# Stick-breaking attention in pairs of heads, dilated units one tile ahead, other banks, constants behind the scratch

## The chip, the cores and the metric

The kernel runs on one core of a Trainium2 chip. Its time is the device time of one execution in microseconds (us); of the kernel before, three runs gave 2281.86, 2284.05 and 2284.53, median 2284.05. TensorE multiplies, VectorE (DVE) and ScalarE (ACT) do the elementwise work and read its results from PSUM, which has 8 banks of 512 fp32 words per partition; weights stream in by DMA.

## The reference

A first block (512 tokens, width 1024; projections, pooling, convolutions, a gated merge) is followed by a second one of two layers. Each layer projects, attends in two ways, merges by gates, and runs a feed-forward network. What the change touches:

```
z    = q @ k.T * scale                        # stick-breaking, 4 heads of 64
keep = where(key < query, log_sigmoid(-z), 0)
attn = where(key < query, exp(log_sigmoid(z) + suffix_sum(keep)), 0)
out  = attn @ v

# dilated: 4 head slots in 3 groups (window, stride) = (128,1), (512,4), (2048,16)
o_g, m_g, den_g = softmax attention of group g
out  = sum_g softmax_g(m_g + log(den_g)) * o_g
x    = x + (gates[:D] * (dil @ w_proj_a) + gates[D:] * (sb @ w_proj_b)) @ w_out
```

## The kernel before, in words

Each fp32 product is made of three fp32r passes: an operand is split into a high part (ScalarE, L453 for weights) and a low part (VectorE, L460), and lines 1597 to 1599 multiply high by high, high by low, low by high. A weight tile of 1024 x 128 is 24 such matmuls of 512 columns (`col_tile`); value projections go by `token_tile` with 48 of 256 columns. The order of the work is written out by hand, and each engine runs its own list in order; semaphores tie them. Weight pieces pass a ring of four slots (`whl`), so tile n + 3 is split while tile n is multiplied. Each layer has 18 tiles for the dilated q, k and v (`DIL_KEYS`, numbered n_ from 0), then 16 gate tiles, then the projections and the output rows. Attention is slipped in between tiles:

- Stick-breaking. Before, one head takes four tiles. Behind tile 0 `sb_scores` (L1807) writes z to banks 2 to 5; `sb_logs` on ScalarE takes abs, exp and log, `sb_softplus` on VectorE adds (L1445) and masks (L1447) them, ScalarE and VectorE split the result (L853, L1451); behind tile 2 `sb_exponents` (L1818) adds triangular sums to z; ScalarE exponentiates; behind tile 4 `sb_values` (L1830) makes the output in bank 6, and `sb_out` splits it into obT (L865, L1456) for `w_proj_b_2`. These fp32 matmuls run as two passes each, so the profile counts two for one.
- Rotation (`rope`, L1427 to L1437 on VectorE) of the 12 q and k tiles, which ScalarE copies out as qraw (L873).
- Dilated. A unit is two heads and 128 queries, eight units per layer, one for two gate tiles: `dil_scores` (L1856, L1860, banks 2 and 3), the maximum, `dil_exp` (L905), `dil_transposes` (L1871, banks 4 and 5), `dil_pT`, `dil_values` (L1889, banks 6 and 7). Groups 1 and 2 are held by class (every fourth token together), group 0 by token.
- `stat_rows` (L1905) turns maxima and denominators into rows, `shift_rows` and `share_rows` make the groups' shares, `share_wide` (L1917) spreads them over partitions, ScalarE copies them (L941), `dil_merge` (L1509 to L1511) applies them, and oaT (L1515) feeds `w_proj_a_2`. Its products are gated from PSUM (L1547), summed (L1549) and split; `row_tiles` then makes the output rows in banks 0 to 3 and 4 to 7.

`take` waits until a bank's last reader, which `give` has noted, is done.

Of the kernel before, what the change touches and what calls it, by code (L numbers as in the profile page):

```python
# [31 lines left out]
P = 128  # L32
D = 1024
SEQ = 512
# [67 lines left out]
def weight_plan():  # L102
# [34 lines left out]
    for l in range(LAYERS):  # L137
# [6 lines left out]
        for g in range(3):  # L144
            add("w_in_2", ("w_in_2v", l, 6 + g), [("dv", l, g, j) for j in range(2)], 1024)
# [12 lines left out]
def build(nc, t, out):  # L158
# [21 lines left out]
    PA_BANK = (2, 3, 4, 5, 0, 1, 6, 7)  # L180
# [3 lines left out]
    SBO = [0, 512, 896, 1152, 1280]  # L184
# [9 lines left out]
    def DIL_KEYS(l):  # L194
        return [(name, l, g, j) for name in ("dq", "dk", "dv") for g in range(3) for j in range(2)]

    count = 0
    for key in W:
# [5 lines left out]
        elif key[0] in ("dq", "dk", "gate"):  # L204
            W_BANK[key] = key[-1] % 2
        elif key[0] == "sv":
            W_BANK[key] = 4
        elif key[0] == "dv":
            W_BANK[key] = 4 if key[2] == 2 else 0
        elif key[0] in ("up_a", "up_b"):  # L210
            W_BANK[key] = (2 * key[2] + (key[0] == "up_b") * 2 - key[2] % 2) % 8


    base = (nc.sbuf_base + 63) // 64 * 64
# [13 lines left out]
    whl = keep("whl", [P, 4, 2, 1024], R)  # L228
    cst_at = at[0]
# [12 lines left out]
    arena = (at[0] + 127) // 128 * 128  # L242

    negtri_r = nc.alloc_sbuf_tensor_at("negtri_r", [P, P], R, offset=tri_at)
    negones_r = nc.alloc_sbuf_tensor_at("negones_r", [P, P], R, offset=vcol_at)

    def over(name, offset, shape, dt=F):
        size = int(np.prod(shape[1:])) * (2 if dt == BF else 4)
        assert arena + offset + size <= top, (name, arena + offset + size - top)
        return nc.alloc_sbuf_tensor_at(name, shape, dt, offset=arena + offset)  # L250

    K = 1024
# [52 lines left out]
    wide = over("wide", 12 * K, [P, 2, 2, SEQ])  # L305
    gates = over("gates", 48 * K, [P, 16, SEQ])
    sbl = over("sbl", 64 * K, [P, 1280])
    sbs = over("sbs", 69 * K, [P, 1280])
    sphi = over("sphi", 64 * K, [P, 1280], R)
    splo = over("splo", 69 * K, [P, 1280], R)  # L310
    sba = over("sba", 74 * K, [P, 1280])
# [32 lines left out]
    with ctx:  # L344
# [5 lines left out]
        def sem(name):  # L350
# [23 lines left out]
        rope_done, z_ps, sb_abs, sb_l, sp_ready, e_ps, sb_attn, sbo_ps, ob_hi, ob_lo = (  # L374
            sem(n) for n in ("rope_done", "z_psum", "sb_abs", "sb_log", "sp_ready", "e_psum", "sb_attn",
# [3 lines left out]
        row_ps, row_x, row_e, den_used, share, wide_ps, wide_in = (  # L379
# [245 lines left out]
        def _(act):  # L625
# [191 lines left out]
            for l in range(LAYERS):  # L817
# [18 lines left out]
                def sb_logs(h):  # L836

                    for kb in range(TB):
                        act.wait_ge(z_ps, 4 * (4 * l + h) + kb + 1)
                        A(sbl[:, SBO[kb]:SBO[kb + 1]], bank(2 + kb)[:, 0:SBO[kb + 1] - SBO[kb]], ACT.Abs).then_inc(sb_abs, 1)  # L840
                    for kb in range(TB):
                        act.wait_ge(sb_abs, 4 * (4 * l + h) + kb + 1)
                        v = sbl[:, SBO[kb]:SBO[kb + 1]]
                        A(v, v, ACT.Exp, scale=-1.0).then_inc(act_chain, 1)
                    chain[0] += 4
                    for kb in range(TB):
                        act.wait_ge(act_chain, chain[0] - 3 + kb)
                        v = sbl[:, SBO[kb]:SBO[kb + 1]]
                        A(v, v, ACT.Ln, bias=1.0).then_inc(sb_l, 1)

                def sb_hi(h):
                    act.wait_ge(sp_ready, 4 * (4 * l + h) + 4)
                    A(sphi[:], sbs[:], ACT.Copy).then_inc(sp_hi, 1)  # L853

                def sb_exp(h):
                    for kb in range(TB):
                        act.wait_ge(e_ps, 4 * (4 * l + h) + kb + 1)
                        if kb == 0 and h:
                            act.wait_ge(sbo_ps, 4 * l + h)
                        A(sba[:, SBO[kb]:SBO[kb + 1]], bank(2 + kb)[:, 0:SBO[kb + 1] - SBO[kb]], ACT.Exp).then_inc(sb_attn, 1)  # L860

                def sb_out(h):
                    act.wait_ge(sbo_ps, 4 * l + h + 1)
                    po = h % 2 * HEAD
                    A(obT[po:po + HEAD, h // 2, 0, :], bank(6)[po:po + HEAD, :], ACT.Copy).then_inc(ob_hi, 1)  # L865

                for n_, key in enumerate(DIL_KEYS(l)):
# [18 lines left out]
                    h, ph = n_ // 4, n_ % 4  # L886
                    if ph == 0 and h >= 1:
                        sb_out(h - 1)
                    if ph == 0 and h < 4:
                        sb_logs(h)  # L890
                    if ph == 1 and h < 4:
                        sb_hi(h)
                    if ph == 2 and h < 4:
                        sb_exp(h)


                def dil_exp(u):
                    j, b = u // 4, u % 4
                    act.wait_ge(max_done, 8 * l + u + 1)
                    if u:  # L900
                        act.wait_ge(pT_ps, 8 * l + u)
                    for e in range(2):
                        for kind, c0, c1 in ((0, 0 if b else P, 256), (1, 256, 512)):
                            h = 2 * j + e
                            ins = A(prob[:, e, c0:c1], bank(2 + e)[:, c0:c1], ACT.Exp, bias=nmax[:, kind, b, h:h + 1],  # L905
                                    accum_out=den[:, kind, b, h:h + 1])
                    ins.then_inc(p_ready, 1)

                def dil_pT(u):
# [1073 lines left out]
```

## Time and profile before

| | us |
|---|---|
| median of 3 runs | 2284.05 |
| profiled execution | 2284.14 |
| its span, first to last instruction | 2282.3 |
| PE busy | 2205.3 |
| DVE busy | 1258.1 |
| ACT busy | 779.2 |

PE is TensorE's matmuls. Their ends are modelled and overlap, so a duration in a row is longer than the step to the next start; the chain of waits gives the steps. Idle time of an engine counts only where another waits for it. The mean granted clock of TensorE is 0.984 of 2.4 GHz.

### The profile page before, as it was taken

How to read it: one execution, taken by the hardware profiler on the slowest of the kernel's cores; microseconds unless marked ns; L12 is line 12 of the kernel's file. 1: busy time of each engine (PE TensorE's matmuls, PEld its weight loads, DVE VectorE, ACT ScalarE, POOL GpSimd, SP SyncE). 2: the span in 40 equal slices, each digit the busy share in tenths (PEclk: the TensorE clock that was granted, in tenths of full speed). 3: DMA queues.
4: the chain of work that ended last, by engine and by line, in shares of the span. 5: the costliest groups of instructions: out<-in, count | busy, mean ns of one | idle time of the engine just before them, and what ended most of it. 6: DMA issues, size and time to landing. Idle time of an engine off the chain costs nothing.

```text
span 2282.3 us, 25769 instructions
## 1 busy us (share of the span) xinstructions
PE 2205.3 (97%) x10730; PEld 1818.5 (80%) x10742; DVE 1258.1 (55%) x1662; ACT 779.2 (34%) x1112; POOL 35.4 (2%) x46
## 2 busy tenths in 40 slices
PE   3999999999999799999999999999999999999998
PEld 2788888888888697877788888889787768888887
DVE  7798797944655746323655554234632365555422
ACT  1223232223442344344343333134434424333211
POOL 1000000000000200000000000000000000000000
PEclk7999999999999899999999999999999989999999
DMA  8332322332222222222223223222222222332222
GB/s 303 116 103 90 108 97 79 111 110 94 88 97 97 74 93 74 90 79 73 74 75 111 92 94 107 86 83 93 74 94 78 69 74 74 101 103 93 95 99 74
DMA packets 188241, 217.91 MB, mean 95 GB/s; under 512 B 3808, under 2 KB 167262, under 8 KB 188126
## 3 DMA queue, kind: packets, MB, share of 16 engines
q1 hardware_dynamic: 184128, 210.52, 27.8%
q10 hardware_dynamic: 3262, 3.60, 0.5%
q8 instruction: 85, 1.39, 0.3%
q0 software_dynamic: 736, 2.15, 0.2%
q14 instruction: 30, 0.25, 0.0%
HBM read 212.06 MB, written 4.19 MB: 95 GB/s over the span
## 4 chain that ended last, share of the span: by engine, by line
PE 91%; DVE 6%; ACT 1%; issue 1%; POOL 0%; DMA 0%; SPq 0%; ACTq 0%; POOLq 0%; DVEq 0%
PE psum L1597 29%; PE psum L1599 28%; PE psum L1598 28%; DVE whl L460 1%; PE psum L1818 1%; DVE adsum L1038 1%; PE psum L1807 1%; PE psum L1830 1%; PE psum L1889 1%; PE psum L1860 1%; PE psum L1871 1%; DMA x<-in_x 0%; PE psum L1917 0%; DVE stat L1007 0%; ACT whl L453 0%
## 5 line engine op out<-in xcount | busy, mean ns | idle before, releaser
L1597 PE MATMUL psum<-hT,whl 128*128 128x512 f32 (+1 forms) x2112 | 804.4, 381 | 8.2 <-DVE hT L1060 5.4
L1598 PE MATMUL psum<-hT,whl 128*128 128x512 f32 (+1 forms) x2112 | 797.0, 377 | 0.0
L1599 PE MATMUL psum<-hT,whl 128*128 128x512 f32 (+1 forms) x2112 | 796.8, 377 | 0.0
L460 DVE TENSOR_TENSOR whl<-raw,whl 128x1024 fp32r<-128x1024 f32 (+1 forms) x368 | 449.3, 1223 | 594.4 <-ACT whl L453 594.4
L453 ACT ACTIVATE whl<-raw 128x1024 fp32r<-128x1024 f32 (+1 forms) x368 | 384.4, 1047 | 468.4 <-PE psum L1599 431.9
L1597 PEld LDWEIGHTS psum<-hT,whl 128*128 128x128 f32 x2112 | 399.0, 189 | 90.3 <-DVE hT L1060 8.9
L1599 PEld LDWEIGHTS psum<-hT,whl 128*128 128x128 f32 x2112 | 399.1, 189 | 73.4
L1598 PEld LDWEIGHTS psum<-hT,whl 128*128 128x128 f32 x2112 | 399.3, 189 | 71.3 <-issue 0.5
L1597 PE MATMUL psum<-whl,ff 128*128 128x512 f32 x352 | 139.2, 395 | 2.2 <-DVE fsil L1576 2.2
L1598 PE MATMUL psum<-whl,ff 128*128 128x512 f32 x352 | 138.9, 395 | 0.0
L1599 PE MATMUL psum<-whl,ff 128*128 128x512 f32 x352 | 138.9, 395 | 0.0
L1597 PE MATMUL psum<-whl,hT 128*128 128x256 f32 (+1 forms) x384 | 124.7, 325 | 10.3 <-DVE gates L1547 6.5
L1598 PE MATMUL psum<-whl,hT 128*128 128x256 f32 (+1 forms) x384 | 123.1, 321 | 0.0
L1599 PE MATMUL psum<-whl,hT 128*128 128x256 f32 (+1 forms) x384 | 123.0, 320 | 0.0
L1101 DVE SCALAR_TENSOR_TENSOR hc<-glu,vcol,hc 128x512 f32<-128x512 f32 x120 | 89.3, 744 | 0.0
L1597 PEld LDWEIGHTS psum<-whl,hT 128*128 128x128 f32 x384 | 73.6, 192 | 17.9 <-DVE gates L1547 7.3
L1567 DVE TENSOR_SCALAR facc<-apad,vcol 128x512 f32<-128x512 f32 x44 | 24.1, 547 | 110.9 <-ACT fsil L970 53.0
L1101 DVE SCALAR_TENSOR_TENSOR acc<-glu,vcol,acc 128x512 f32<-128x512 f32 x112 | 83.3, 744 | 0.1
L1597 PEld LDWEIGHTS psum<-whl,ff 128*128 128x128 f32 x352 | 66.3, 188 | 18.2 <-issue 3.0
L1598 PEld LDWEIGHTS psum<-whl,ff 128*128 128x128 f32 x352 | 66.3, 188 | 15.4
L1599 PEld LDWEIGHTS psum<-whl,ff 128*128 128x128 f32 x352 | 66.3, 188 | 15.4
L1599 PEld LDWEIGHTS psum<-whl,hT 128*128 128x128 f32 x384 | 73.7, 192 | 5.3
(270 smaller groups left out, 2159.4 us busy)
## 6 DMA issues: line engine op xcount, KB each, us to landing
raw<-in_w_in SPq DMA_DIRECT2D x88, 1024.0 KB, 5.1
raw<-in_w_up SPq DMA_DIRECT2D x44, 1024.0 KB, 5.1
raw<-in_w_down SPq DMA_DIRECT2D x20, 1024.0 KB, 5.1
ada<-in_w_ada SPq DMA_DIRECT2D x12, 1024.0 KB, 10.0
raw<-in_w_branch SPq DMA_DIRECT2D x12, 1024.0 KB, 5.1
raw<-in_w_out SPq DMA_DIRECT2D x12, 1024.0 KB, 5.0
x<-in_x SPq DMA_DIRECT2D x4, 512.0 KB, 6.7
v_by_token<-vnat ACTq DMA_DIRECT2D x4, 512.0 KB, 2.8
```

Of the source, the lines that this page charges most:

```text
L453: nc.scalar.activation(whl_view(w, 0), raw_view(w), ACT.Copy).then_inc(w_hi, 1)
L460: nc.vector.tensor_tensor(whl_view(w, 1), raw_view(w), whl_view(w, 0).bitcast(F), ALU.subtract).then_inc(w_lo, 1)
L1038: ins = V.scalar_tensor_tensor(o_, at_k(k), cact[:, k:k + 1], o_, ALU.mult, ALU.add)
L1101: last[dst is acc1] = step(V.scalar_tensor_tensor(A_(dst), g[:, k:k + SEQ], col("cf_w", 8 * k + tt), A_(dst), ALU.mult, ALU.add))
L1567: link(V.tensor_scalar(facc[:], apad[:, j, 2:2 + SEQ], cw(2), col("conv_b", FT * l + f), ALU.mult, ALU.add))
L1597: M(out_, stat_hi, mov_hi, start=start, stop=False, **kw)
L1598: M(out_, stat_hi, mov_lo, start=False, stop=False, **kw)
L1599: return M(out_, stat_lo, mov_hi, start=False, stop=stop, **kw)
L1807: M(bank(2 + kb)[:, 0:SEQ - kb * P], sbk[rows, h // 2, kb * P:(kb + 1) * P], sbq[rows, h // 2, kb * P:], start=True, stop=True, skip_group ...
L1818: M(bank(2 + kb)[:, (jb - kb) * P:SEQ - kb * P], (negtri_r if jb == kb else negones_r)[:], part[:, SBO[jb]:SBO[jb + 1]], start=False, stop ...
L1830: ins = M(bank(6)[po:po + HEAD, kb * P:], sbv[:, kb, h * HEAD:(h + 1) * HEAD], sba[:, SBO[kb]:SBO[kb + 1]], start=kb == 0, stop=kb == TB - ...
L1860: ins = M(bank(2 + e)[:, a:z], qd[heads, g, j, b * P:(b + 1) * P], kd[heads, g, j, k0:k0 + z - a], start=False, stop=g == 2, skip_group_ch ...
```

## The change

Stick-breaking heads go in pairs. `sb_scores(p)` issues both heads of pair p in turn, block by block, head 0 to banks 2 to 4 and head 1 to banks 5 to 7, with the four blocks packed into 1280 words (the 128-wide one ahead of the 256-wide one). ScalarE and VectorE work on one head's 1280 words at once instead of four blocks, with scratch of its own for each of the two. `sb_values(p)` issues both heads in turn to bank 2, one to partitions 0 to 63 and one to 64 to 127, and obT is split once for both. Pair p starts behind tile 7p: scores at 7p, exponents at 7p + 4 and 7p + 5, values at 7p + 6.

The value tensors of the dilated groups come in the order 1, 2, 0 (loads too) and use banks 0 and 1, 3 and 4, 6 and 7. The first dilated unit's scores come behind tile 16, and then every unit runs one tile earlier: values behind the even gate tile, the next transposes and the scores after those behind the odd one. Values of groups 1 and 2 and their statistics are written in token order (every fourth word), so VectorE no longer reorders. `stat_rows` is split in two. The shares are multiplied straight from PSUM, and the merge stands ahead of a weight split. `PA_BANK` starts with 2, 3, 0, 1. In SBUF the constants move behind the scratch area.

```diff
-        for g in range(3):
+        for g in (1, 2, 0):
             add("w_in_2", ("w_in_2v", l, 6 + g), [("dv", l, g, j) for j in range(2)], 1024)
...
-    PA_BANK = (2, 3, 4, 5, 0, 1, 6, 7)
+    PA_BANK = (2, 3, 0, 1, 4, 5, 6, 7)
-    SBO = [0, 512, 896, 1152, 1280]
+    SBO = [0, 512, 1024, 896]
+    SBW = [512, 384, 256, 128]
+    Z_BANK = (2, 5)
...
-            W_BANK[key] = 4 if key[2] == 2 else 0
+            W_BANK[key] = (6, 0, 3)[key[2]]
...
+    arena = at[0]
+    at[0] += ARENA
     cst_at = at[0]
...
                 def sb_logs(h):
...
+                    e = h % 2
+                    act.wait_ge(z_ps, 4 * l + h + 1)
+                    link(A(sbl[e][:], psum[:, Z_BANK[e] * SEQ:Z_BANK[e] * SEQ + 1280], ACT.Abs))
+                    link(A(sbl[e][:], sbl[e][:], ACT.Exp, scale=-1.0))
+                    A(sbl[e][:], sbl[e][:], ACT.Ln, bias=1.0).then_inc(sb_l, 1)
...
+                def sb_out(p):
+                    act.wait_ge(sbo_ps, 2 * l + p + 1)
+                    A(obT[:, p, 0, :], bank(2), ACT.Copy).then_inc(ob_hi, 1)
...
+                    for p in range(2):
+                        ph = n_ - 7 * p
+                        if ph in (0, 1):
+                            sb_logs(2 * p + ph)
+                        if ph in (2, 3):
+                            sb_hi(2 * p + ph - 2)
+                        if ph in (4, 5):
+                            sb_exp(2 * p + ph - 4)
+                        if ph == 7:
+                            sb_out(p)
...
-                for j in range(2):
-                    act.wait_ge(wide_ps, 2 * l + j + 1)
-                    A(wide[:, j, :, :].rearrange("p a b -> p (a b)"), psum[:, (2 + 2 * j) * SEQ:(4 + 2 * j) * SEQ], ACT.Copy).then_inc(wide_in, 1)
...
+                    link(V.scalar_tensor_tensor(sbs[e][:], psum[:, Z_BANK[e] * SEQ:Z_BANK[e] * SEQ + 1280], 0.0, sbl[e][:], ALU.max, ALU.add))
...
+                def sb_out(p):
+                    dve.wait_ge(ob_hi, 2 * l + p + 1)
+                    V.tensor_tensor(obT[:, p, 1, :], bank(2), obT[:, p, 0, :].bitcast(F), ALU.subtract).then_inc(ob_lo, 1)
...
+                        if ph in (1, 2):
+                            sb_softplus(2 * p + ph - 1)
+                        if ph in (3, 4):
+                            sb_lo(2 * p + ph - 3)
+                        if ph == 7:
+                            sb_out(p)
...
+                    take(*range(2, 8))
+                    for kb in (0, 1, 3, 2):
+                        for e in range(2):
+                            rows = slice(e * HEAD, (e + 1) * HEAD)
+                            c0 = Z_BANK[e] * SEQ + SBO[kb]
+                            ins = M(psum[:, c0:c0 + SBW[kb]], sbk[rows, p, kb * P:(kb + 1) * P], sbq[rows, p, kb * P:],
+                                    start=kb != 3, stop=True, skip_group_check=True)
...
                     ins.then_inc(sbo_ps, 1)
-                    give(6, ob_lo, 4 * l + h + 1)
...
+                    give(2, ob_lo, 2 * l + p + 1)
...
+                            o_ = bank(6 + c // 2)[e * HEAD:(e + 1) * HEAD, :]
+                            o_ = o_[:, b * P:(b + 1) * P] if c < 2 else by_token(o_)[:, b, :]
...
+                for u in range(8):
                     col_tile(("gate", l, 2 * u), h_at(0), h_at(1))
+                    dil_values(u)
+                    if u == 7:
+                        stat_rows(1, den)
+                    col_tile(("gate", l, 2 * u + 1), h_at(0), h_at(1))
                     if u < 7:
+                        dil_transposes(u + 1)
+                    if u < 6:
+                        dil_scores(u + 2)
+                    if u == 6:
+                        stat_rows(0, nmax)
```

TensorE before, behind tile 4 of layer 0: the values of head 0 (L1830) and the scores of head 1 (L1807).

```order
L1599 MATMUL psum<-hT,whl 128x512
L1830 MATMUL psum<-sba,sbv 64x512 [waits sb_attn,act_read,h_gained]
L1830 MATMUL psum<-sba,sbv 64x384 [waits sb_attn]
L1830 MATMUL psum<-sba,sbv 64x256 [waits sb_attn]
L1830 MATMUL psum<-sba,sbv 64x128 [waits sb_attn]
L1807 MATMUL psum<-sbq,sbk 128x512 [waits sb_attn,act_read]
L1807 MATMUL psum<-sbq,sbk 128x384 [waits sb_attn]
L1807 MATMUL psum<-sbq,sbk 128x256 [waits sb_attn]
L1807 MATMUL psum<-sbq,sbk 128x128 [waits sb_attn]
L1597 MATMUL psum<-hT,whl 128x512 [waits w_lo,act_read]
```

TensorE now, behind tile 6 of layer 0: the values of the first pair (L1844; `sba_121` is head 0's, `sba_122` head 1's).

```order
L1606 MATMUL psum<-hT,whl 128x512
L1844 MATMUL psum<-sba_121,sbv 64x512 [waits sb_attn,act_read]
L1844 MATMUL psum<-sba_122,sbv 64x512
L1844 MATMUL psum<-sba_121,sbv 64x384
L1844 MATMUL psum<-sba_122,sbv 64x384
L1844 MATMUL psum<-sba_121,sbv 64x256
L1844 MATMUL psum<-sba_122,sbv 64x256
L1844 MATMUL psum<-sba_121,sbv 64x128
L1844 MATMUL psum<-sba_122,sbv 64x128
L1604 MATMUL psum<-hT,whl 128x512 [waits w_lo,act_read]
```

And behind tile 7 the scores of the second pair (L1815).

```order
L1606 MATMUL psum<-hT,whl 128x512
L1815 MATMUL psum<-sbq,sbk 128x512 [waits sb_attn,ob_lo,act_read]
L1815 MATMUL psum<-sbq,sbk 128x512
L1815 MATMUL psum<-sbq,sbk 128x384 x2
L1815 MATMUL psum<-sbq,sbk 128x128 x2
L1815 MATMUL psum<-sbq,sbk 128x256 x2
L1604 MATMUL psum<-hT,whl 128x512 [waits w_lo,act_read]
```

The two heads alternate in both, and the second pair's scores have `ob_lo`, the low half of the output, among their waits, which no scores had.

ScalarE now at the same place: copy of tile 7 (L902), high half of the output (L865), then the next pair's logs.

```order
L461 ACTIVATE whl<-raw 128x1024 [waits w_used,raw_in0]
L902 ACTIVATE qraw<-psum 128x512 [waits rope_done,w_used]
L865 ACTIVATE obT<-psum 128x512 [waits sbo_psum]
L848 ACTIVATE sbl_113<-psum 128x1280 [waits z_psum]
L849 ACTIVATE sbl_113<-sbl_113 128x1280 [waits act_chain]
L850 ACTIVATE sbl_113<-sbl_113 128x1280 [waits act_chain]
```

The output's high half stood before in the same way behind the copy of a tile; now the bank that it reads is one that scores take.

VectorE before, between the products of `w_proj_b_2` (L1541) and of `w_proj_a_2`.

```order
L460 TENSOR_TENSOR whl<-raw,whl 128x1024 [waits w_hi]
L1509 TENSOR_TENSOR osb_108<-osb_108,wide 128x512 [waits o_copied,wide_copied]
L1510 TENSOR_TENSOR osb_108<-osb_108,wide 128x512
L1511 TENSOR_TENSOR wide<-osb_108 128x512 [waits dve_chain]
L1509 TENSOR_TENSOR osb_109<-osb_109,wide 128x512 [waits o_copied,wide_copied]
L1510 TENSOR_TENSOR osb_109<-osb_109,wide 128x512
L1511 TENSOR_TENSOR wide<-osb_109 128x512 [waits dve_chain]
L1515 TENSOR_TENSOR oaT<-wide,oaT 128x512 [waits oa_hi] x2
```

And now.

```order
L1496 TENSOR_TENSOR osb_108<-osb_108,psum 128x1024 [waits o_copied,wide_psum]
L1499 TENSOR_TENSOR wide<-osb_108 128x512 [waits wide_copied]
L1496 TENSOR_TENSOR osb_109<-osb_109,psum 128x1024 [waits o_copied,wide_psum]
L1499 TENSOR_TENSOR wide<-osb_109 128x512 [waits wide_copied]
L468 TENSOR_TENSOR whl<-raw,whl 128x1024 [waits w_hi]
L1503 TENSOR_TENSOR oaT<-wide,oaT 128x512 [waits oa_hi] x2
```

Six instructions became four, they read PSUM, and the weight split went behind them.

## Rows read from the trace of the kernel before

**Rows 1.** Page of the run: busy times by engine; chain that ended last

```profile
PE 2205.3 (97%) x10730; PEld 1818.5 (80%) x10742; DVE 1258.1 (55%) x1662; ACT 779.2 (34%) x1112; POOL 35.4 (2%) x46
...
PE 91%; DVE 6%; ACT 1%; issue 1%; POOL 0%; DMA 0%; SPq 0%; ACTq 0%; POOLq 0%; DVEq 0%
```

**Rows 2.** All waits of PE: engine, line waited for: total us, times, longest

```profile
PE psum L1597 <- DVE gates L1547: 6.5, 2, 4.1
...
PE psum L1597 <- DVE oaT L1515: 3.1, 2, 2.2
PE psum L1597 <- ACT vd L882: 2.3, 2, 1.2
...
PE psum L1597 <- ACT qraw L873: 1.5, 2, 0.7
```

**Rows 3.** Chain of waits, 861 to 876 us: start, us, what

```profile
862.18 2.30 PE psum L1830 x8
864.48 2.35 PE psum L1807 x8
866.83 0.43 PE psum L1597
...
867.97 0.23 PE psum L1598
```

**Rows 4.** Stretches: length, busy us of each engine, then granted clock

```profile
1103.00:1108.00 5.00, 4.91 (x14) 3.88 (x15) 4.97 (x9) 0.34 (x2) 0.00 (x0) 0.66 0.08 9
1834.00:1842.00 8.00, 8.00 (x20) 5.42 (x19) 4.70 (x6) 2.65 (x4) 0.00 (x0) 0.57 0.00 1
1860.00:1866.00 6.00, 5.98 (x17) 4.72 (x18) 5.72 (x9) 2.74 (x4) 0.00 (x0) 0.60 0.01 3
```

**Rows 5.** Chain of waits, 970 to 998 us, dilated units

```profile
971.88 1.08 PE psum L1860 x12
...
978.64 0.81 PE psum L1889 x12
...
993.26 1.02 PE psum L1889 x16
```

**Rows 6.** Chain of waits, 1088 to 1094 us, the shares' matmuls

```profile
1090.02 3.77 PE psum L1917 x8
```

**Rows 7.** Timeline of DVE, 832 to 858 us

```profile
839.42 0.69 DVE L1445 SCALAR_TENSOR_TENSOR sbs<-psum,sbl 128x512 f32<-128x512 f32 x1 [6.91 <-ACT sbl L849]
...
842.34 1.22 DVE L460 TENSOR_TENSOR whl<-raw,whl 128x1024 fp32r<-128x1024 f32 x1
...
843.48 0.75 DVE L1427 STREAM_SHUFFLE rot<-qraw 128x512 f32<-128x512 f32 x1
...
846.04 1.48 DVE L1451 TENSOR_TENSOR splo<-sbs,sphi 128x1280 fp32r<-128x1280 f32 x1
...
855.58 1.11 DVE L1437 TENSOR_TENSOR qd<-rot 128x512 f32<-128x512 f32 x1
```

**Rows 8.** Timeline, 1111 to 1120 us, around the start of the output rows

```profile
1111.65 0.68 DVE L1547 SCALAR_TENSOR_TENSOR gates<-gates,psum 128x512 f32<-128x512 f32 x1
...
1117.77 0.68 DVE L1547 SCALAR_TENSOR_TENSOR gates<-gates,psum 128x512 f32<-128x512 f32 x1
...
1118.56 0.47 PE L1597 MATMUL psum<-whl,hT 128*128 128x512 f32 x1 [2.48 <-DVE gates L1547]
```

**Rows 9.** Timeline, 862 to 866 us: start, us, engine, line [idle before]

```profile
862.22 0.60 ACT L873 ACTIVATE qraw<-psum 128x512 f32<-128x512 f32 x1 [3.89 <-PE psum L1599]
...
864.52 0.59 ACT L865 ACTIVATE obT<-psum 64x512 fp32r<-64x512 f32 x1 [1.70 <-PE psum L1830]
...
865.14 0.68 DVE L1456 TENSOR_TENSOR obT<-psum,obT 64x512 fp32r<-64x512 f32 x1 [2.62 <-ACT obT L865]
```

**Rows 10.** Timeline of ACT, 832 to 858 us

```profile
843.26 1.26 ACT L853 ACTIVATE sphi<-sbs 128x1280 fp32r<-128x1280 f32 x1
844.42 1.05 ACT L453 ACTIVATE whl<-raw 128x1024 fp32r<-128x1024 f32 x1
```

More of the change, by code:

```diff
@@ L304, in build @@
     mrow = over("mrow", 0, [P, 6, SEQ])
-    wide = over("wide", 12 * K, [P, 2, 2, SEQ])
+    wide = over("wide", 12 * K, [P, 2, SEQ])
     gates = over("gates", 48 * K, [P, 16, SEQ])
[L307 to L311, printed above, removed]
+    sb_at = (64, 48)
+    sbl = [over(f"sbl{e}", sb_at[e] * K, [P, 1280]) for e in range(2)]
+    sbs = [over(f"sbs{e}", (sb_at[e] + 5) * K, [P, 1280]) for e in range(2)]
+    sphi = [over(f"sphi{e}", sb_at[e] * K, [P, 1280], R) for e in range(2)]
+    splo = [over(f"splo{e}", (sb_at[e] + 5) * K, [P, 1280], R) for e in range(2)]
+    sba = [over(f"sba{e}", (sb_at[e] + 10) * K, [P, 1280]) for e in range(2)]
     oaT = over("oaT", 80 * K, [P, 2, 2, SEQ], R)
@@ L851, in sb_hi @@
+                    A(sbl[e][:], sbl[e][:], ACT.Ln, bias=1.0).then_inc(sb_l, 1)
                 def sb_hi(h):
[L852 to L853 removed]
+                    act.wait_ge(sp_ready, 2 * (4 * l + h) + 2)
+                    A(sphi[h % 2][:], sbs[h % 2][:], ACT.Copy).then_inc(sp_hi, 1)
                 def sb_exp(h):
[L856 to L860, printed above, removed]
@@ new lines, in sb_exponents @@
+                def sb_exponents(h):
+                    e = h % 2
+                    pe.wait_ge(sp_lo, 4 * l + h + 1)
+                    for kb in range(TB):
+                        c0 = Z_BANK[e] * SEQ + SBO[kb]
+                        for jb in range(kb, TB):
+                            for part in (sphi[e], splo[e]):
+                                M(psum[:, c0 + (jb - kb) * P:c0 + SBW[kb]], (negtri_r if jb == kb else negones_r)[:],
+                                  part[:, SBO[jb]:SBO[jb] + SBW[jb]], start=False, stop=False, skip_group_check=True)
+                        ins = M(psum[:, c0:c0 + P], identb[:], sbaddb[:], start=False, stop=True, skip_group_check=True)
+                    ins.then_inc(e_ps, 1)
+                    for b in range(Z_BANK[e], Z_BANK[e] + 3):
+                        give(b, sb_attn, 4 * l + h + 1)
@@ new lines, in sb_values @@
+                def sb_values(p):
+                    take(2)
+                    if p == 0:
+                        await_read(pe, ("sv", l, 1))
+                    pe.wait_ge(sb_attn, 4 * l + 2 * p + 2)
+                    for kb in range(TB):
+                        for e in range(2):
+                            h = 2 * p + e
+                            ins = M(bank(2)[e * HEAD:(e + 1) * HEAD, kb * P:], sbv[:, kb, h * HEAD:(h + 1) * HEAD],
+                                    sba[e][:, SBO[kb]:SBO[kb] + SBW[kb]], start=kb == 0, stop=kb == TB - 1, skip_group_check=True)
+                    ins.then_inc(sbo_ps, 1)
+                    give(2, ob_lo, 2 * l + p + 1)
```

308 lines of the change are left out of this document (133 added, 175 removed).

## The prediction

> **What bounds the kernel now.** I read the page first, then the waits of TensorE, then the chain of waits in the two attention stretches, then the clock by stretches. TensorE is busy 97% of the span and is 91% of the chain that ended last [rows 1]; all other engines matter only where TensorE waits for them, or where they make it wait after the change. Inside the code that changes it waits 13.4 us over both layers (6.5 + 3.1 + 2.3 + 1.5) [rows 2]. The chain of waits shows what one head costs: its values run 2.30 us and the scores of the next head 2.35 us, and the first tile matmul behind them takes 0.43 us to the next start where others take 0.23 [rows 3], so each excursion out of the tiles costs 0.2 us more. A tile is 24 such matmuls, 5.5 us. Three stretches have a mean granted clock of 0.66, 0.57 and 0.60: behind the wait for L1515 at 1101 us, behind the shares' matmuls of layer 1, and behind the longest wait [rows 4]; the clock has the levels 1.2 and 2.4 GHz, so these are stretches partly at 1.2.
>
> **Scores and values in turn.** A head has four of each, 512, 384, 256 and 128 columns wide, and every fp32 matmul runs as two passes (x8 in the row). Counted in passes of 128 columns, a head is 20 and took 2.30 to 2.35 us, 0.115 a step. Scores use 64 partitions of the array, values 64 of its columns, so two heads don't share cells, but before they come one head after the other. The dilated units already take two heads in turn: scores of 16 steps in 1.08 us, values of 12 and 16 steps in 0.81 and 1.02 us [rows 5]. Serial they would need 1.84, 1.38 and 1.84. If matmuls start in program order and a pass waits only for the last one of its own head, I can lay them out: the second pass of head 0 covers the first of head 1, the second of head 1 covers the next first of head 0. That gives 10, 7 and 9 steps of 0.107 us (128 columns, 2 cycles each, at 2.4 GHz; an estimate that these rows bear out): 1.07, 0.75, 0.96, against 1.08, 0.81, 1.02. The same layout for the new order (512, 384, 128, 256 for scores, 512 to 128 for values) gives 25 and 24 steps: 2.7 and 2.6 us, with the rows' rest of 0.01 to 0.06 about 2.75 and 2.65. Two heads cost 4.70 and 4.60 before. So 1.95 us less for each, with four pairs in two layers: **7.8 + 7.8 = 15.6 us**. Bounds: 0 if they don't overlap, 18.6 if they overlap wholly.
>
> The Trainium skill ("TensorE: Matmul & The Clock Gate", Part 3 on row and column tiling) gives the span of packed matmuls as one matmul plus some 4 ns per further tile, which would be the whole overlap, 18.6 us; the trace disagrees, since 1.08 us is more than half of 1.84, and the layout above stands.
>
> The exponent matmuls keep number and width, so they cost the same. One excursion fewer per layer (8 instead of 9 up to the last value tile; 17 in the dilated part both times) at 0.2 us: **0.4 us**.
>
> **Waits that go.** Row L873 (1.5 us) and L882 (2.3 us): the first value tile reused banks 0 and 1 while ScalarE still read them. Now a whole exponent block lies ahead of it, and the three value tensors have banks of their own. L1515 (3.1 us): ScalarE's copies of the shares go, and VectorE multiplies out of PSUM ahead of its weight split. The shares' matmuls run 3.77 us [rows 6], the first half is there after 1.9; a merge is a product of 1024 and a sum of 512 elements, by L1451 (1.48 us for 1280) and L1445 (0.69 for 512) [rows 7] about 1.9 us; two of them, a split of 1.15 and the two low halves of 0.75 end at 1.9 + 3.8 + 1.15 + 1.5 = 8.3, that is 4.6 us behind the shares' matmuls and inside the 5.5 us of the next projection tile. L1547 (6.5 us): the output rows start at 1118.56 after 2.48 us of wait, when VectorE has read the sixth product, L1547 at 1117.77, from bank 1 [rows 8]. With the new bank order the four banks that the output rows take hold products 0 to 3, and the fourth was read from 1111.65 to 1112.3 [rows 8], 3.7 us before TensorE is there. What is late next is the low half of product 2, wanted 5.5 us after the start, about when VectorE ends product 5: no wait. **13.4 us** in all; bounds 10 and 13.4.
>
> **Clock.** Without the waits at 1101 and 1856 the low stretches behind them should go. A mean of 0.66 over 5 us is 5 x 0.34 / 0.5 = 3.4 us at half speed, and costs half of that, 1.7 us; 0.60 over 6 us is 4.8, and costs 2.4 [rows 4]: **4.1 us**; bounds 0 and 4.1. The stretch behind the shares' matmuls (8 x 0.43 / 0.5 = 6.9 us low, 3.4 lost) stays, since these stay.
>
> **Waits that come.** (1) The values of a pair now land in bank 2, and the second pair's scores want banks 2 to 7, bank 2 included. It is free when VectorE has made the low half of the output. Both ScalarE and VectorE reach that only behind the copy of tile 7, the very tile whose end TensorE is at. From the same steps of before: copy at +0.11, next copy 0.5 later, 0.59 long, then VectorE 0.68 [rows 9], then the start on TensorE: 2.0 us of wait, in each layer: 4.0 us. Behind it on TensorE stand the scores and every later tile; no other engine is held by it. Before, scores used banks 2 to 5, values bank 6, and nothing of this was on the path. Bounds 3.4 and 4.6 (by the latencies).
> (2) The exponents of a pair's first head come four tiles after the scores, with a longer chain ahead. From the scores' start: ScalarE starts at +2.8 (head 0's last score) and makes three passes of 1280 at 1.26, a weight split 1.05 [rows 10]: 7.6. VectorE: split (1.14 to the next start, 842.34 to 843.48), rotation 2.56 (843.48 to 846.04), softplus. The latter took 2.92 in eight pieces (839.42 to 842.34) [rows 7], and I take 2.3 in three: 13.6. ScalarE's second head ends its split at 13.85, so VectorE goes on there: split, rotation, softplus 19.9, split, rotation (+0.4 for the strided form, 1.11 us [rows 7]) 24.0, low half 1.48 [rows 7]: 25.4. TensorE is there at 2.75 + 4 x 5.53 = 24.9: 0.5 us of wait. The second pair has two strided rotations ahead: 0.9 us. Two layers: 2.8 us; bounds 0 (softplus at 2.0) and 6 (softplus at 2.9, 0.6 more for each head of four pairs). The second head's exponents come a tile later and are ready.
> Together **6.8 us**, and 1 us for one or two of these waits that bring the clock down as the one at 1101 did.
>
> **The rest costs nothing.** Fewer ScalarE and VectorE instructions lie beside TensorE's tiles. In the dilated part the probabilities now have two tiles of time instead of one, and the transposed ones one (needed 2.0 us, given 5.5). The row statistics are split, the same 16 matmuls; the shares' rows on VectorE start at the same tile as before and are fewer. Value tiles are reordered with their loads. Constants behind the scratch change addresses alone; tile matmuls on operands in many places all run at 0.23, so I give this nothing.
>
> **Sum.** 15.6 + 0.4 + 13.4 + 4.1 - 6.8 - 1.0 = 25.7. The profiled execution took 2284.14 us, 0.1 from the median of 2284.05: 2284.1 - 25.7 = **2258.4 us**. Its own range 2250 to 2266.
>
> **Rivals.**
> *Strided results.* The values of groups 1 and 2 and half of the statistics now write every fourth word of PSUM; no matmul of before does, so no row prices it. Nearest are VectorE's strided writes, 1.11 against about 0.69 us (rotation), 1.6 times. At twice the time, the 0.53 us of a unit's strided passes grow by 0.53 in 16 units (8.5) and the statistics' 16 strided passes by 1.8 a layer (3.6): +12.1, 2270. Against it: a fp32 pass delivers one column per 0.83 ns, slow already. I take nothing and 10% for this case. The Trainium skill ("PSUM — Partial Sum Buffer", Specifications) says that any non-contiguous access slows matmuls significantly, without a factor; no run here shows it, and by it this case holds.
> *Slower than before:* the same place, if a strided pass takes over 3.1 times as long: each further unit costs 12.1, and 25.7 / 12.1 = 2.1. At four times: 2258 + 36 = 2294. 4%.
> *No overlap of pairs*: the sum without 15.6, 2274. Against it stand the dilated rows. 3%.
> *VectorE's chain slips by a tile* in each of the four pairs, if its in-order splits hold it: 4 x 5.5, 2280, counted as half no change. 4%.
> *Each of the six new waits brings a low clock,* 1.7 us each as behind 1101: +10, 2268. Against it: the wait of 2.48 us at the output rows of layer 0 [rows 8] was not followed by one. 6%.
> *The forecast* has 73%. Range for 8 in 10: 2250 to 2272. A difference under 0.2% (4.6 us) can't be told from none. Faster 94%, same 2%, slower 4%.
>
> **What would show it.** Scores of a pair at 2.7 to 2.8 us and values at 2.6 to 2.7 in the chain; no wait of TensorE for gates, oaT, vd or qraw; a wait of about 2 us for obT ahead of the second scores of each layer, and one of 0.3 to 1.5 for splo ahead of the pairs' first exponents; the clock low only behind the shares' matmuls; values of a unit still 1.02. Wrong would be: units' values at 1.3 or more, a wait at the output rows, or a wait for splo over 2 us.

## The result, and the profile after

| | before | after |
|---|---|---|
| median, us | 2283.06 (2281.86 to 2284.53, 4 runs) | 2244.57 (2243.1 to 2246.91, 4 runs) |
| profiled execution, us | 2284.14 | 2243.10 |
| its span, us | 2282.3 | 2240.9 |

The ratio is 0.9832, 95% interval 0.9815 to 0.9849. The change is worth 38.5 us by the medians and 41.0 by the profiled executions; 25.7 were forecast, and 2244.57 lies below the range of 2250 to 2272.

The page of the kernel after, busy times and the shares of the chain that ended last, answers to [rows 1]:

```profile
PE 2168.8 (97%) x10742; PEld 1805.2 (81%) x10742; DVE 1248.9 (56%) x1612; ACT 763.7 (34%) x1008; POOL 35.4 (2%) x46
...
PE 89%; DVE 6%; ACT 2%; issue 2%; DMA 1%; POOL 0%; SPq 0%; POOLq 0%; ACTq 0%; DVEq 0%
```

TensorE is as much the bound as before. It is busy for 36.5 us less for about the same number of matmuls, so most of what went was not idle time. The waits of TensorE (engine, line waited for, total us, times, longest) answer to [rows 2]:

```profile
PE psum L1628 <- ACT xn L788: 12.5, 2, 9.6
...
PE psum L1604 <- DVE hT L1064: 5.5, 3, 4.4
PE psum L1815 <- issue: 4.1, 2, 2.1
PE psum L1828 <- DVE splo L1455: 2.7, 4, 0.8
```

No row is left for gates, oaT, vd or qraw. Two are new: 2.05 us twice ahead of the scores (L1815), and splo ahead of the pairs' first exponents (L1828). The first has no engine's name. The timeline of all engines at that place (start, us, engine, line, idle before) names it:

```profile
881.46 0.60 ACT L902 ACTIVATE qraw<-psum 128x512 f32<-128x512 f32 x1 [6.42 <-PE psum L1606]
881.96 0.59 ACT L865 ACTIVATE obT<-psum 128x512 fp32r<-128x512 f32 x1
882.58 0.69 DVE L1459 TENSOR_TENSOR obT<-psum,obT 128x512 fp32r<-128x512 f32 x1 [3.73 <-ACT obT L865]
...
883.48 1.09 PE L1815 MATMUL psum<-sbq,sbk 64*128 64x512 f32 x3 [2.05 <-issue]
```

ScalarE copies tile 7, then the output of the pair; VectorE makes the low half, and the scores start at 883.48, 0.9 us behind its start. That is the wait forecast from [rows 9], with its size. The chain of waits in the same attention stretch (start, us, what) answers to [rows 3]:

```profile
831.19 2.36 PE psum L1815 x16
...
856.07 1.50 PE psum L1828 x8
...
864.90 1.23 PE psum L1828 x8
...
873.46 2.30 PE psum L1844 x16
...
883.48 2.43 PE psum L1815 x16
...
926.65 2.31 PE psum L1844 x16
```

A pair's scores take 2.36 us (2.43 behind the wait) and its values 2.30. One head took 2.35 and 2.30 in [rows 3]: the second head costs nothing. The last thing to see there is the first block of exponents: 1.50 us behind a wait for splo, 1.23 where there is none. The timeline of TensorE shows why:

```profile
855.16 0.39 PE L1606 MATMUL psum<-hT,whl 128*128 128x512 f32 x1
856.07 0.50 PE L1828 MATMUL psum<-sphi,negtri_r 128*128 128x512 f32 x1 [0.52 <-DVE splo L1455]
856.41 0.40 PE L1828 MATMUL psum<-splo,negtri_r 128*128 128x512 f32 x1
```

The row of waits counts 0.52 us, from the end of the last tile matmul. But without a wait the next matmul starts 0.23 us behind the start of the last one and not 0.39, and the first matmul behind the wait takes 0.34 to the next start instead of 0.23. So this wait costs 0.16 + 0.11 = 0.27 us more than its row says, at a granted clock of 1.00. The dilated unit with strided results, in the chain of waits, stands as in [rows 5]:

```profile
975.97 1.02 PE psum L1893 x16
```

The clock needs a fuller account than [rows 4] gave. A stretch of T us at mean clock c loses T x (1 - c). All stretches of before between the first scores and the end of layer 1's mix with a clock under 1 (length, busy us of each engine, clock, DMA share, GB/s):

```profile
1092.00:1108.00 16.00, 13.85 (x42) 9.74 (x41) 11.99 (x17) 5.24 (x7) 0.00 (x0) 0.79 0.04 10
1832.00:1844.00 12.00, 11.61 (x31) 7.27 (x29) 6.59 (x9) 4.48 (x6) 0.00 (x0) 0.72 0.13 48
1856.00:1868.00 12.00, 7.98 (x25) 6.40 (x26) 10.71 (x15) 3.61 (x6) 0.00 (x0) 0.72 0.01 1
```

By this formula they lose 3.4 us each, 10.2 in all. But in the third the clock is low from 1858.0 on, and TensorE waits until 1860.02:

```profile
1858.00:1860.00 2.00, 0.00 (x0) 0.01 (x1) 1.94 (x4) 0.63 (x1) 0.00 (x0) 0.50 0.00 0
```

```profile
1860.02 0.76 PE L1597 MATMUL psum<-whl,hT 128*128 128x512 f32 x1 [4.06 <-DVE gates L1547]
```

A low clock costs nothing while TensorE waits, so this stretch costs 2.4 us, the figure that [rows 4] gave, and the three together 9.2. Those of after:

```profile
1080.00:1088.00 8.00, 8.00 (x25) 5.53 (x24) 7.63 (x10) 1.27 (x2) 0.00 (x0) 0.79 0.03 9
1800.00:1812.00 12.00, 12.00 (x32) 7.16 (x31) 8.56 (x12) 2.31 (x3) 0.00 (x0) 0.72 0.22 84
```

They lose 1.7 and 3.4 us, 5.1 in all, and TensorE works through both. So the clock gave back 4.1 us, as forecast.

What is left is in no wait and in no line that the change touches. Matmuls of w_down (ff is the streamed operand) in layer 1 of before and of after (count, duration in ns, first and last start):

```profile
L1597 PE MATMUL psum<-whl,ff x176: 390/393/468, 2152.3 to 2274.4; 128*128 128x512 f32 x176
```

```profile
L1604 PE MATMUL psum<-whl,ff x176: 389/389/467, 2113.9 to 2233.0; 128*128 128x512 f32 x176
```

From the first to the last of this line lie 525 matmuls: 122.1 us before, 119.1 after, 0.2326 and 0.2269 us a step. The same in the merge of the first block, where yahl, also in the scratch, is the stationary operand:

```profile
L1597 PE MATMUL psum<-yahl,whl x64: 392/394/398, 473.5 to 550.3; 128*128 128x512 f32 x64
```

```profile
L1604 PE MATMUL psum<-yahl,whl x64: 388/389/390, 474.3 to 549.8; 128*128 128x512 f32 x64
```

The stretch, 76.8 us before and 75.5 after, holds other tiles too. The mean step from one start to the next is 232 to 234 ns before and 226 to 228 after for the matmuls whose operand lies in the scratch (yahl, ybhi, ychi, mhi and their low parts, obT, oaT, ff), and 227 in both for hT, which lies elsewhere. The 768 matmuls of the merge by 6.5 ns are 5.0 us, the 1056 of w_down by 5.7 ns are 6.0 us, and the 192 on obT and oaT by about 5 ns are 1.0 us: 12.0 us in all. (The expectations below count 720 matmuls in the merge and leave out the last 192, and so say 10.7.)

First starts of TensorE's lines, by stage, show where the 41.4 us of span went:

| stage | before | after | shorter | forecast |
|---|---|---|---|---|
| start to first scores | 834.6 | 831.1 | 3.5 | 0 |
| scores to shares, layer 0 | 255.3 | 246.8 | 8.5 | 6.0 |
| shares to w_down, layer 0 | 318.7 | 311.6 | 7.1 | 13.7 in both layers |
| w_down to next scores | 167.2 | 164.4 | 2.8 | 0 |
| scores to shares, layer 1 | 255.2 | 246.8 | 8.4 | 6.0 |
| shares to w_down, layer 1 | 321.3 | 313.2 | 8.1 | (above) |
| w_down to the end | 130.0 | 127.0 | 3.0 | 0 |

Three stages in which no instruction changed give 9.3 us. That was the question for the experiments.

### The profile page after: what moved, and what is told of

It reads as the page before. It is cut to its first block, busy times and chain, and to the rows that moved or that the text cites. A ratio compares the mean times of both kernels' runs of the same rounds, so it can differ in the third digit from the quotient of the medians.

```text
span 2240.9 us, 25627 instructions
## 1 busy us (share of the span) xinstructions
PE 2168.8 (97%) x10742; PEld 1805.2 (81%) x10742; DVE 1248.9 (56%) x1612; ACT 763.7 (34%) x1008; POOL 35.4 (2%) x46
## 4 chain that ended last, share of the span: by engine, by line
PE 89%; DVE 6%; ACT 2%; issue 2%; DMA 1%; POOL 0%; SPq 0%; POOLq 0%; ACTq 0%; DVEq 0%
PE psum L1604 28%; PE psum L1605 28%; PE psum L1606 28%; PE psum L1828 1%; DVE whl L468 1%; DVE adsum L1042 1%; PE psum L1861 1%; PE psum L1893 1%; PE psum L1873 1%; PE psum L1815 0%; PE psum L1844 0%; DMA x<-in_x 0%; DVE stat L1011 0%; PE psum L1920 0%; POOL stat L618 0%
## 5 line engine op out<-in xcount | busy, mean ns | idle before, releaser
L1604 PE MATMUL psum<-whl,ff 128*128 128x512 f32 x352 | 137.3, 390 | 2.2 <-DVE fsil L1583 2.2
L1606 PE MATMUL psum<-whl,ff 128*128 128x512 f32 x352 | 137.0, 389 | 0.0
L1605 PE MATMUL psum<-whl,ff 128*128 128x512 f32 x352 | 137.0, 389 | 0.0
L1606 PEld LDWEIGHTS psum<-whl,ff 128*128 128x128 f32 x352 | 66.1, 188 | 13.7
L1605 PEld LDWEIGHTS psum<-whl,ff 128*128 128x128 f32 x352 | 66.1, 188 | 13.7
```

The lines of the kernel that those rows point to most:

```text
L1604: M(out_, stat_hi, mov_hi, start=start, stop=False, **kw)
L1605: M(out_, stat_hi, mov_lo, start=False, stop=False, **kw)
L1606: return M(out_, stat_lo, mov_hi, start=False, stop=stop, **kw)
```

## Experiments

**The scratch in other places.** Theory A: the step of a tile matmul depends on where its operand in the scratch stands. Rival B: the time saved in those stages comes from something else, and the steps are a by-product. In before hT and the weights stand at 128 modulo 512 and the scratch at 0; in after all stand at 128.

Before, scratch 128 bytes further:

```diff
-    arena = (at[0] + 127) // 128 * 128
+    arena = (at[0] + 127) // 128 * 128 + 128
```

> The kernel before with its scratch area 128 bytes further on in SBUF (start 128128 instead of 128000 bytes, 128 instead of 0 modulo 512); nothing else changed. Theory A (where a streamed operand starts against the weights and hT, which start 128 modulo 512, sets the pace of a matmul): tile matmuls on operands in the scratch fall from a step of 232 to 234 ns to 226.7, as in the changed kernel; 720 of them in the merge and 1056 on ff give 4.7 + 6.0 = 10.7 us less, ratio 0.9953. Theory B (it was the absolute place, or traffic of other engines, not the alignment): step stays at 232 to 234 ns, time the same within 0.1%.

After, scratch 384 bytes further, at 0 as it was:

```diff
-    arena = at[0]
-    at[0] += ARENA
+    arena = at[0] + 384
+    at[0] += ARENA + 384
```

> The changed kernel with its scratch area 384 bytes further on (start 115200, 0 modulo 512), weights and hT as they are, constants moved by the same 384. Theory A: the step of matmuls on scratch operands rises from 226.7 to 232 to 234 ns, 10.7 us more, some 2255 us (ratio to the kernel before 0.988). Theory B: step and time as the changed kernel, ratio 0.983.

Before, everything at 0:

```diff
-    base = (nc.sbuf_base + 63) // 64 * 64
+    base = (nc.sbuf_base + 63) // 64 * 64 + 384
...
-    arena = (at[0] + 127) // 128 * 128
+    arena = (at[0] + 511) // 512 * 512
```

> The kernel before with everything in SBUF 384 bytes further on and the scratch at the next multiple of 512: x, hT, raw, weights and scratch all start 0 modulo 512. If the offset between streamed operand and weights counts (A1), all tile matmuls step at 226.7 ns and the time falls by 10.7 us, ratio 0.995. If the streamed operand's own start at 0 modulo 512 is what slows (A2), all of the some 8800 tile matmuls of 512 columns step at 232 to 234 ns: 50 to 60 us more, ratio 1.02 to 1.03.

Measured, beside a before of 2284.2 us: 2276.34 (ratio 0.9963, 0.9951 to 0.9976) for the first; 2254.54 for the second (0.9872, 0.9858 to 0.9885), where the kernel after had 0.9832; 2274.51 for the third (0.9954, 0.9939 to 0.9969). The row of w_down in each, in this order:

```profile
L1597 PE MATMUL psum<-whl,ff x176: 389/389/467, 2145.4 to 2264.5; 128*128 128x512 f32 x176
```

```profile
L1604 PE MATMUL psum<-whl,ff x176: 390/393/472, 2122.1 to 2244.1; 128*128 128x512 f32 x176
```

```profile
L1597 PE MATMUL psum<-whl,ff x176: 389/389/467, 2146.9 to 2266.0; 128*128 128x512 f32 x176
```

The stretches are 119.1, 122.0 and 119.1 us. Moving addresses takes the slow step out of the kernel before, or brings it back into the kernel after, and 8 to 10 us of time go with it. Theory A holds, B falls. The third also shows that a multiple of 512 is not slow by itself: what counts is how far the scratch stands from the weights. Four more placements, all in the kernel before, show which distances are slow:

```diff
-    arena = (at[0] + 127) // 128 * 128
+    arena = (at[0] + 127) // 128 * 128 + 64
```

the same with + 256 and with + 384, and all that is kept 256 bytes further with the scratch back on a multiple of 512.

> The kernel before with the scratch 64 bytes further, at 64 modulo 512, while hT and the weights stand at 128 modulo 512. One look at the steps of the tile matmuls in the merge (yahl, 192 of them) and of the last projection (ff). Theory: only where the streamed operand and the weights stand at the same offset modulo 512 is the step 226.7 ns, so here it is 231 to 236, as in the kernel before. Rival: the operand's own multiple of 512 is what is slow, and any other place gives 226.7.

> The kernel before with the scratch 256 bytes further, at 256 modulo 512, weights at 128: they differ by 128. Theory: 231 to 236 ns a step. Rival, the operand's own multiple of 512 is what is slow: 226.7.

> The kernel before with the scratch 384 bytes further, at 384 modulo 512, weights at 128: they differ by 256. Theory with a period of 512: 231 to 236 ns a step. If the period is 256 and not 512: 226.7.

> The kernel before with all that is kept (hT and the weights too) 256 bytes further, at 384 modulo 512, and the scratch at 0 modulo 512: they differ by 128, as in the kernel with the scratch 256 bytes further, but in other places. Theory, the difference alone counts: the same step for the scratch operands as there, and 226.7 for hT, which moves with the weights. Rival, the place of one operand counts: a step unlike it, or hT's changes as well.

The rows of w_down for + 64, + 256, + 384 and the moved base:

```profile
L1597 PE MATMUL psum<-whl,ff x176: 394/394/473, 2153.4 to 2273.6; 128*128 128x512 f32 x176
```

```profile
L1597 PE MATMUL psum<-whl,ff x176: 390/393/471, 2150.0 to 2272.1; 128*128 128x512 f32 x176
```

```profile
L1597 PE MATMUL psum<-whl,ff x176: 387/389/467, 2147.6 to 2266.8; 128*128 128x512 f32 x176
```

```profile
L1597 PE MATMUL psum<-whl,ff x176: 390/393/472, 2152.3 to 2274.3; 128*128 128x512 f32 x176
```

The distances to the weights modulo 256 are 192, 128, 0 and 128, and the stretches 120.2, 122.1, 119.2 and 122.0 us. The two at 128 are slow in different places and alike, which bears out that the difference counts. My period of 512, in the expectations, was wrong: the kernel with 384 more differs by 256 from the weights and is fast, so the period is 256 as far as these places show. At 192 w_down stands between, at 228.9 ns a step, while yahl keeps the slow 76.8 us:

```profile
L1597 PE MATMUL psum<-yahl,whl x64: 394/394/394, 474.3 to 551.1; 128*128 128x512 f32 x64
```

The same kernel has one operand that tells more. poolhl starts 64 bytes beside a multiple of 256 within the scratch, so here its distance is 0 where yahl's is 192:

```profile
L1597 PE MATMUL psum<-poolhl,whl x16: 389/389/389, 115.3 to 419.2; 128*128 128x512 f32 x16
```

Its mean step is 226.7 ns, next to 233 of yahl in one kernel. In the kernel before, where poolhl stands at 192, it is 233, and in the kernel after, where it stands at 64, it is 231: the change left these 48 matmuls slower than they can be. So the distance of the operand counts, and not something else that a moved scratch changes. The time from the start to the first scores agrees over all kernels of this case: 829.8 to 831.3 us in the eight whose scratch stands at 0 from the weights, 834.4 to 835.3 in the six where it stands at 128 or 192.

The times of these four kernels, one execution each (2283.4, 2281.8, 2276.5 and 2284.1, before 2286.0) go the same way, the fast one 5 to 8 us below the others. Why the distance matters, no run here shows.

**The heads of a pair in turn or not.** The kernel after, with one head behind the other inside scores and values:

```diff
-                    for kb in (0, 1, 3, 2):
-                        for e in range(2):
+                    for e in range(2):
+                        for kb in (0, 1, 3, 2):
...
-                    for kb in range(TB):
-                        for e in range(2):
+                    for e in range(2):
+                        for kb in range(TB):
```

> The changed kernel with the two heads of a pair one after the other in scores and in values (the loop over heads outside the loop over blocks), same banks, same waits. If the pairs' overlap is whole, as the 2.36 and 2.30 us in the changed kernel's chain say, scores and values of a pair go back to 4.65 us each: 8 x 2.3 = 18.6 us more, some 2263 us, ratio 0.991. The forecast's step count of 25 and 24 would give only 15.6.

2262.43 us (2257.87 to 2263.78), ratio 0.9901 (0.9887 to 0.9914). The chain of waits:

```profile
830.45 3.97 PE psum L1815 x15
...
874.30 2.30 PE psum L1844 x8
876.70 1.46 PE psum L1844 x6
878.16 0.43 PE psum L1604
```

The scores take 3.97 us to the next tile and the values 3.86 (874.30 to 878.16), against 2.36 and 2.30. The second head costs 1.6 us here and not 2.3, since its first matmuls start while the last ones of the first head still run. Four pairs by 1.61 and 1.56 are 12.7 us. The other part of the 18.2 between the profiled executions is clock: behind the wait at the second pair's scores of layer 0 there is now a stretch that the kernel after doesn't have,

```profile
884.00:900.00 16.00, 14.12 (x39) 9.52 (x40) 6.11 (x9) 5.67 (x6) 0.00 (x0) 0.68 0.19 63
```

5.1 us lost, and over all stretches 11.9 against 5.1. The two parts are 12.7 + 6.8 = 19.5 us, 1.3 more than measured; 0.7 of that is an earlier first score (830.45 against 831.19), the rest is open. So the order of the heads is worth 12.7 us by itself. The expectation had 2263 us, and 2262 came out, but by luck: it took all of the difference for overlap, 18.6 us.

**The new waits.** The kernel after, with the output of a pair ahead of tile 7's copy and rotation on ScalarE and VectorE, and the low halves of the softplus ahead of the rotation; then each alone.

```diff
                     split_hi(W[key] + 3)
+                    if n_ in (7, 14):
+                        sb_out(n_ // 7 - 1)
...
-                        if ph == 7:
-                            sb_out(p)
...
                     split_lo(W[key] + 3)
+                    if n_ in (7, 14):
+                        sb_out(n_ // 7 - 1)
+                    if n_ < 14 and n_ % 7 in (3, 4):
+                        sb_lo(2 * (n_ // 7) + n_ % 7 - 3)
                     if 1 <= n_ <= 12:
                         rope(n_ - 1)
...
-                        if ph in (3, 4):
-                            sb_lo(2 * p + ph - 3)
...
-                        if ph == 7:
-                            sb_out(p)
```

> The kernel after with two reorderings: ScalarE's and VectorE's two halves of a pair's output come right behind the weight split of tile 7, ahead of the copy and the rotation; VectorE's low halves of the softplus come ahead of the rotation of the same tile. My theory: the waits of 4.1 us at L1815 (the profile names no engine there) are the wait for obT's low half, which both engines reach only behind tile 7's copy, and those of 2.7 us at L1828 are the wait for splo behind one rotation of 2.56 us. Then both rows go from TensorE's waits, 6.5 to 7 us in all, and the time is 2237 to 2239 us, ratio to the kernel before 0.980. Rival 1: the 2.05 us at L1815 are not obT but the issue of the matmuls or the wait for banks 5 to 7 (exponents read by ScalarE): they stay, 2241.5. Rival 2: what is late next takes their place (the softplus of the second head), 2243, no gain.

> The kernel after with the two halves of a pair's output right behind the weight split of tile 7 on ScalarE and VectorE, ahead of the copy and the rotation, and nothing else. My theory: the row of 4.1 us at L1815 goes or falls below 0.5, that of 2.7 at L1828 stays within 1 us: 4 us faster than the kernel after, ratio 0.981 to 0.982. Rival: the row stays at 4.1 and the time at 2243 to 2245.

> The kernel after with VectorE's low halves of the softplus ahead of the rotation of the same tile, and nothing else. My theory: the row of 2.7 us at L1828 goes, that of 4.1 at L1815 stays: 2 to 3 us faster than the kernel after. Rival: the chain is bound by ScalarE's three passes for the second head, and the wait moves to the second head's exponents: no gain.

Both: 2232.69 us (2231.65 to 2234.74), ratio 0.9778 (0.9765 to 0.9792) beside a before of 2284.26, the fastest kernel of this case. The rows of TensorE's waits between which the two would stand:

```profile
PE psum L1604 <- DVE hT L1064: 6.1, 4, 4.4
PE psum L1604 <- DVE fsil L1583: 2.2, 2, 1.1
```

Both rows are gone. The chain of waits, and its one stretch of low clock past the first scores:

```profile
830.91 2.36 PE psum L1815 x16
...
855.28 1.23 PE psum L1828 x8
...
872.40 2.31 PE psum L1844 x16
...
880.37 2.36 PE psum L1815 x16
```

```profile
1792.00:1800.00 8.00, 8.00 (x23) 5.20 (x22) 7.08 (x9) 1.33 (x3) 0.00 (x0) 0.79 0.14 54
```

The first exponents are back at 1.23 us, and 1.7 us are lost to the clock where the kernel after lost 5.1. By spans: 4.1 + 2.7 of waits, 4 x 0.27 that the waits for splo cost beside their row, and 3.4 of clock are 11.3 of the 11.4 us from 2240.9 to 2229.5. The stages agree: each layer is 4.0 us shorter between scores and shares, and 1.6 behind the shares. I had expected 6.5 to 7 us, waits alone.

The output alone: 2237.8 us (0.98, 0.9787 to 0.9813). The low halves alone: 2238.84 (0.9805, 0.9791 to 0.9818). In each the other wait stays, the first row from the output's kernel and the second from the other:

```profile
PE psum L1828 <- DVE splo L1455: 2.6, 4, 0.8
```

```profile
PE psum L1815 <- issue: 4.1, 2, 2.1
```

Their spans are 4.6 and 3.6 us shorter than after's, and each lost the same 5.1 us to the clock as after. Only with both together is there no stretch behind the shares of layer 0 and a shorter one in layer 1, 3.4 us less. That the two moves did this isn't shown: the shares come 170 us behind the last of these waits, and the kernel after with its scratch 384 bytes further, which keeps every one of the waits, has no such stretch in layer 0 either:

```profile
1080.00:1096.00 16.00, 16.00 (x62) 11.19 (x61) 13.98 (x20) 3.81 (x5) 0.00 (x0) 1.00 0.25 70
```

It has one at 1613 us instead, behind the wait of the second pair's scores in layer 1, which take 3.79 us there and not 2.43. So which stretches of low clock a kernel gets differs between kernels that issue the same instructions.

**The order of the banks alone.** The kernel before with `PA_BANK` of after:

```diff
-    PA_BANK = (2, 3, 4, 5, 0, 1, 6, 7)
+    PA_BANK = (2, 3, 0, 1, 4, 5, 6, 7)
```

> The kernel before with the banks of the first projection's products in the order of the kernel after (2, 3, 0, 1, 4, 5, 6, 7), and nothing else. My theory: the wait of TensorE for VectorE at the output rows (L1547, 6.5 us over both layers) goes, and with it the low clock behind the one of layer 1 (2.4 us by the rows): 7 to 9 us faster than the kernel before, ratio 0.996 to 0.997. Rival: VectorE's products are late whatever the bank, the wait comes back at the low half of the mix (mixed_lo) with the same size: ratio 1.000.

2274.21 us (2273.37 to 2275.23), ratio 0.996 (0.9947 to 0.9974): 10.0 us. Its list of TensorE's waits where the row for gates stood, and two stretches of the clock:

```profile
PE psum L1706 <- DVE vcol L1025: 6.7, 1, 6.7
PE psum L1597 <- DVE hT L1060: 5.9, 4, 4.4
PE psum L1597 <- DVE oaT L1515: 2.8, 2, 1.5
```

```profile
1092.00:1108.00 16.00, 14.69 (x47) 10.18 (x46) 11.58 (x16) 4.83 (x6) 0.00 (x0) 0.79 0.00 1
1856.00:1868.00 12.00, 12.00 (x55) 9.94 (x54) 9.77 (x13) 4.81 (x6) 0.00 (x0) 1.00 0.23 78
```

The row for gates, 6.5 us, is gone and nothing stands in its place. The stretch at 1856 is at full clock, which is worth the 2.4 us that the low clock cost TensorE there. Two waits gone are some 0.5 us beside their rows, as behind splo, and the row for oaT is 0.3 shorter: 9.7 of the 9.9 us between the spans. The theory's 7 to 9 had the first two terms. A number in a table of banks is a quarter of the whole gain.

## Why the prediction was wrong

**The failed step** is the last of "the rest costs nothing": "Constants behind the scratch change addresses alone; tile matmuls on operands in many places all run at 0.23, so I give this nothing." It is worth 12.0 us by the steps, 8 to 10 by the medians of three kernels that move addresses and nothing else. 0.23 is a number with two digits: 0.2267 and 0.2326 both read as 0.23, and the difference meets some 2000 matmuls. The other terms, as measured, come to 30.4 us by the sum below, which would have been 2253.7 and inside the range. The profile of before had the two levels; they show in a count by operand over a long stretch, as in the rows of ff above, and not in single steps.

**A term mis-sized: scores and values in turn.** 15.6 us forecast. A pair takes 2.36 and 2.30 and not 2.75 and 2.65, so the whole 18.6, less what the two scores behind a wait take more (2.43): 18.4. The layout in which the second head waits for a pass of the first fitted 1.08, 0.81 and 1.02 of [rows 5]. So does another, which I didn't try: whole overlap and a fixed part of a block. 8 passes of 128 columns by 0.107 are 0.85, and 0.22 more is 1.08, 0.17 more is 1.02. The same fixed part stands in the single head of [rows 3]: 20 by 0.107 is 2.13, and it took 2.35 and 2.30. Two models fitted three rows, and the fourth, the one head, could have told them apart before the run: the layout makes it 20 steps of 0.107, 2.13, and leaves 0.2 us without a reason. The Trainium skill ("TensorE: Matmul & The Clock Gate", Part 3 on row and column tiling), which has packed matmuls span one matmul and some 4 ns, was set aside in the prediction; here the rows of after agree with it, 2.30 for two heads against 2.30 for one.

**Waits that go, 13.4:** right in each of the four, and the bank order is shown alone. What was named as late next, the low half of product 2, made no wait. What the prediction had nowhere is the cost beside the row. The eight waits that went had it too: ahead of each the last matmul's 0.16 us of overlap was lost, and the first one behind took 0.07 to 0.13 longer to the next start. That is some 2.0 us in all, an estimate from the starts at these eight places.

**Clock, 4.1 less 1.0:** 4.1 in the trace. The stretches behind 1101 and 1856 went; the row at 1092 to 1108 holds the shares' stretch and the wait's together. The charge of 1 us for the new waits was not due in the profiled execution, by luck as much as by reason: with the scratch moved, and with the heads one behind the other, a low stretch stands behind one of these waits (1613 and 887 us). Another 1.1 us was due, which I had nowhere: 4 x 0.27 beside the rows of splo. The forecast that the shares' matmuls keep their low clock is right for both layers here.

**Waits that come, 6.8:** 4.1 + 2.7, right in place and size, and each shown by taking it away.

**The rest costs nothing:** strided results 0, right: 1.02 as before. The Trainium skill ("PSUM — Partial Sum Buffer", Specifications) has any non-contiguous access slow matmuls significantly; for fp32 passes that write every fourth word the trace disagrees, and the rival built on it is out, with the one at four times. The rivals of no overlap and of a chain slipped by a tile are out by the rows of the chain. That of a low clock at each new wait is out by the stretches of after, where none of the six has one.

Sum: 18.4 + 0.4 + 13.4 + 2.0 + 4.1 - 6.8 - 1.1 + 12.0 = 42.4. The waits ahead of the first scores (adsum, vstage, xn and vcol, by the two lists of waits) are 2.3 us longer in after, which leaves 40.1 of the 41.4 us between the spans. The 0.4 for one excursion fewer in each layer was not measured apart, and 1.3 us stay open. The medians are 38.5 apart and the profiled executions 41.0, since the profiled run of after was its fastest.

## What to carry to other kernels

Give an address a price: compare the step of the same matmul by operand over a hundred or more of them, and where two levels show, place the operands at a multiple of 256 bytes from each other. Before believing a model of overlap that fits the small blocks, ask it for the block that has no overlap. Count a wait of TensorE higher than its row, here by a quarter of a microsecond, and charge a low clock only for the time in which TensorE works. And order an output's release ahead of work that nobody waits for: two such moves were worth 11.4 us here, 7.9 of it in the waits, their cost beside the rows included.

## What the runs showed of the hardware

- A tile matmul of 128x512 steps at 227 ns where the scratch operand stands 0 modulo 256 bytes from the weights, at 232 to 234 where it stands at 128, at 229 (ff) or 233 (yahl, poolhl) at 192, and at 231 (poolhl) at 64; seen in nine placements of the kernels before and after, for both the streamed and the stationary operand.
- Matmuls on 64 partitions of the array, and on 64 columns, overlap wholly with those on the other 64: 2.36 and 2.30 us for two heads, issued in turn. Issued head by head they still overlap at the joint (3.97 and 3.86, not 4.70 and 4.60).
- A wait of TensorE costs more than its row: 0.16 us of overlap between two matmuls is lost, and the first one behind it takes 0.34 us to the next start and not 0.23, at a granted clock of 1.00.
- The clock fell to 1.2 GHz within 6 us of the start of the shares' matmuls, which use 4 of the 128 partitions, in 25 of the 28 places (14 kernels, two layers), and each of these stretches cost 1.7 to 3.4 us. Where it fell differed between kernels with the same instructions.
